# Hybrid decoder step on one core: a stacked fp32r product for the samples' new states in scan groups 2 to 4, weight halves made by ScalarE at a tile's begin, the gate's root at a tile's end

## What is computed

```
def ssd_scan(x, dt, A, B, C, h0):
    cum = jnp.cumsum(dt * A, axis=2)
    ...
    decay_to_end = jnp.exp(cum[:, :, -1:] - cum)
    chunk_states = jnp.einsum('bcjgn,bcjgr,bcjgrp->bcgrpn', B, decay_to_end * dt, x)
    chunk_decay = jnp.exp(cum[:, :, -1])
    def step(h, inp):
        d, s = inp
        return d[..., None, None] * h + s, h
```

```
    g = y.reshape(b, l, D_SSM) * jax.nn.silu(z.astype(jnp.float32))
    g = g.reshape(b, l, SSD_GROUPS, D_SSM // SSD_GROUPS)
    g = g * lax.rsqrt(jnp.mean(g * g, axis=-1, keepdims=True) + EPS)
```

## Time and profile before

| | us |
|---|---|
| median of 3 runs | 1800.54 (1800.42 to 1800.7) |
| profiled execution | 1800.39 |
| its span in the profile | 1798.8 |
| PE busy in the span | 1779.2 |
| DVE busy | 1088.6 |
| ACT busy | 770.2 |
| the 16 scan tiles, roughly | 546 to 755 of the span |

### The profile page before, as it was taken

The page is one execution under the profiler, slowest core; times in us unless marked ns, Lnnn a source line. Parts: engine busy times, 40 slices in busy tenths (PEclk is TensorE's granted clock), DMA queues, the critical chain, the costliest instruction groups (busy, mean ns, idle before and its releaser), DMA issues.

```text
span 1798.8 us, 34945 instructions
## 1 busy us (share of the span) xinstructions
PE 1779.2 (99%) x13213; PEld 1746.5 (97%) x13213; DVE 1088.6 (61%) x2004; ACT 770.2 (43%) x1139; POOL 453.2 (25%) x352
## 2 busy tenths in 40 slices
PE   8999999999999999999999999999999999999998
PEld 7999999999998898899899999999999999999998
DVE  5577887999788787865875333443434434344444
ACT  6443435555356565633443333333333333333442
POOL 1577776777651122222100000000000000000132
PEclk9999999999999999999999999999999999999999
DMA  8665554555545555564335444444444454444442
GB/s 252 176 189 153 145 157 139 149 152 153 153 144 165 161 177 163 163 215 152 117 123 166 156 140 140 157 156 155 140 140 153 156 158 140 140 151 158 154 143 87
DMA packets 287354, 278.42 MB, mean 155 GB/s; under 512 B 11639, under 2 KB 284767, under 8 KB 286385
## 3 DMA queue, kind: packets, MB, share of 16 engines
q1 hardware_dynamic: 249112, 247.87, 45.4%
q10 hardware_dynamic: 36496, 21.77, 4.1%
q0 software_dynamic: 1648, 7.43, 1.3%
HBM read 261.25 MB, written 17.22 MB: 155 GB/s over the span
## 4 chain that ended last, share of the span: by engine, by line
PE 94%; ACT 2%; DVE 2%; DMA 0%; issue 0%; ACTq 0%; SPq 0%; DVEq 0%
PE ps L1804 28%; PE ps L1806 28%; PE ps L1805 28%; PE ps L1863 1%; PE ps L2087 1%; PE ps L1865 1%; PE ps L1864 1%; PE ps L2060 1%; PE ps L2037 1%; PE ps L2131 1%; PE ps L2132 1%; PE ps L2133 1%; DMA xn<-in_x_prompt 0%; DVE mix L1671 0%; ACT wgt L988 0%
## 5 line engine op out<-in xcount | busy, mean ns | idle before, releaser
L1804 PE MATMUL ps<-ahi,whi 128*128 128x320 f32 x2304 | 717.8, 312 | 0.0
L1806 PE MATMUL ps<-ahi,wlo 128*128 128x320 f32 x2304 | 711.9, 309 | 0.0
L1805 PE MATMUL ps<-alo,whi 128*128 128x320 f32 x2304 | 711.8, 309 | 0.0
L677 ACT ACTIVATE whi<-raw 128x1024 fp32r<-128x1024 f32 (+1 forms) x467 | 479.5, 1048 | 448.6 <-PE ps L1806 382.9
L1205 DVE TENSOR_TENSOR wlo<-raw,whi 128x1024 fp32r<-128x1024 f32 x347 | 424.2, 1245 | 242.4 <-ACT whi L677 239.7
L1804 PEld LDWEIGHTS ps<-ahi,whi 128*128 128x128 f32 x2304 | 432.5, 188 | 1.7
L1805 PEld LDWEIGHTS ps<-alo,whi 128*128 128x128 f32 x2304 | 432.6, 188 | 0.5
L1806 PEld LDWEIGHTS ps<-ahi,wlo 128*128 128x128 f32 x2304 | 432.5, 188 | 0.0
L1804 PE MATMUL ps<-hhi,whi 128*128 128x320 f32 x1016 | 314.3, 309 | 0.0
L1806 PE MATMUL ps<-hhi,wlo 128*128 128x320 f32 x1016 | 313.9, 309 | 0.0
L1805 PE MATMUL ps<-hlo,whi 128*128 128x320 f32 x1016 | 313.9, 309 | 0.0
(11 more groups left out here) (316 smaller groups left out, 1626.3 us busy)
## 6 DMA issues: line engine op xcount, KB each, us to landing
raw<-in_w_in SPq DMA_DIRECT2D x144, 512.0 KB, 3.7
raw<-in_w_up SPq DMA_DIRECT2D x128, 512.0 KB, 4.5
raw<-in_w_down SPq DMA_DIRECT2D x128, 512.0 KB, 4.5
raw<-in_w_out SPq DMA_DIRECT2D x64, 512.0 KB, 3.8
h<-in_state_ssm ACTq DMA_DIRECT2D x16, 512.0 KB, 4.9
out<-hout ACTq DMA_DIRECT2D x16, 512.0 KB, 3.2
x_transposed<-xt ACTq DMA_DIRECT2D x1, 2560.0 KB, 10.1
xr<-x_transposed POOLq DMA_DIRECT2D x1, 2560.0 KB, 9.9
```

Of the source, the lines that this page charges most:

```text
L677: act.activation(whi[:, kq, :, 0:width], raw[:, kq, :, 0:width], ACT.Copy).then_inc(hi_done, 1)
L1804: pe.matmul(out, wh, hi[:, kk, :], start=(kk == 0), stop=False)
L1805: pe.matmul(out, wh, lo[:, kk, :], start=False, stop=False)
L1806: last = pe.matmul(out, wl, hi[:, kk, :], start=False, stop=(kk == NT - 1))
```

## The change

Four things change.

1. **The product.** For i ≥ 1 the samples' new states are formed by two fp32r matmuls with all 128 rows of contraction instead of two fp32 matmuls with 32 rows. The rows are stacked: `xq[h]` holds in rows 64 to 127 the high part of `xdd` (a rounded copy, ACT), in rows 32 to 63 the unrounded `xdd` of its half (ACT), in rows 0 to 31 the low part (a subtraction, DVE). `bq` holds, against these, the masked B, its low part and its high part. Each tile makes its `xq` (four ACT activations, two DVE subtractions); the `bq` of a group is made during the group before it, by ACT: `b_rows` at j = 1, `b_masked` (8 activations) at j = 2, `b_low` and `b_high` (8 and 2) at j = 3, with one subtraction by DVE at j = 2 and one more transpose on PE at j = 1. DVE's `bm` falls away for i ≥ 1.
2. **The weights.** From tile 1 on, ACT makes both high halves of a tile one behind the other at the tile's begin; before, the second came after the old states' copies. DVE's second low half stays where it was, and the two new subtractions stand behind it.
3. **The gate.** ACT copies the mean away (`gate_keep`) where it took the root, PE waits for that copy only, and `gate_root` moves behind the tile's second Exp. The early load of the root's table (`expect_root`) falls away here.
4. **The staging.** PE reads x and B from `xb` itself; `xst` and `bt` are gone.

```diff
@@ ACT @@
-            def stage_x(T):
...
-            def stage_b(i):
...
+            def b_rows(transposed):
+                act.activation(bts[64:P, :], transposed, ACT.Copy)
+                act.activation(bthi[64:P, :], transposed, ACT.Copy).then_inc(bts_ready, 1)
+
+            def b_masked(i):
+                act.wait_ge(bts_ready, i)
+                for b in range(NB):
+                    last = act.activation(bq[i % 2][64:P, b, :], bts[64:P, :], ACT.Copy, scale=blk[64:P, b:b + 1])
+                last.then_inc(bq_rows, 1)
+
+            def b_low(i):
+                act.wait_ge(btlo_done, i)
+                for b in range(NB):
+                    own = slice(64 + 32 * (b // 4), 96 + 32 * (b // 4))
+                    last = act.activation(bq[i % 2][32:64, b, :], btlo[own, :], ACT.Copy, scale=blk[own, b:b + 1])
+                last.then_inc(bq_ready, 1)
+
+            def b_high(i):
+                act.wait_ge(bq_rows, i)
+                for h in range(2):
+                    own = slice(64 + 32 * h, 96 + 32 * h)
+                    last = act.activation(bq[i % 2][0:32, 4 * h:4 * h + 4, :],
+                                          bq[i % 2][own, 4 * h:4 * h + 4, :].bitcast(F32), ACT.Copy)
+                last.then_inc(bq_ready, 1)
...
+            def gate_keep(g):
+                act.wait_ge(gn_mm, g + 1)
+                act.activation(gss[:, g, :], ps[:, 5, 0:TOK], ACT.Copy).then_inc(gn_kept, 1)
+
             def gate_root(g):
-                expect_root()
-                act.wait_ge(gn_mm, g + 1)
-                act.activation(gss[:, g, :], ps[:, 5, 0:TOK], ACT.Sqrt, bias=eps[:, 0:1], scale=float(GROUPS)
+                act.wait_ge(gn_kept, g + 1)
+                act.activation(gss[:, g, :], gss[:, g, :], ACT.Sqrt, bias=eps[:, 0:1], scale=float(GROUPS)
                                ).then_inc(rooted, 1)
...
                     ahead(Q_WC, i, 2 * j)
+                    if not first:
+                        ahead(Q_WC, i, 2 * j + 1)
...
+                    if i:
+                        act.wait_ge(xd_ready, T + 1)
+                        act.wait_ge(st_done, T)
+                        for h in range(2):
+                            act.activation(xq[h][64:P, :], xdd[64:P, 2, :], ACT.Copy).then_inc(xhi_done, 1)
+                        for h in range(2):
+                            last = act.activation(xq[h][32:64, :], xdd[64 + 32 * h:96 + 32 * h, 2, :], ACT.Copy)
+                        last.then_inc(xq_ready, 1)
...
                     if j == 1 and i >= 1:
-                        gate_root(i - 1)
-                    ahead(Q_WC, i, 2 * j + 1)
+                        gate_keep(i - 1)
...
                     decay(T, 1)
+                    if j == 1 and i < 3:
+                        act.wait_ge(bts_trans, i + 1)
+                        b_rows(ps[64:P, 3, TOK:448])
...
+                    if j == 1 and i >= 1:
+                        gate_root(i - 1)
+                    if j == 2 and i < 3:
+                        b_masked(i + 1)
+                    if j == 3 and i < 3:
+                        b_low(i + 1)
+                        b_high(i + 1)
                     store_h(T)
@@ DVE @@
+                    if j == 2 and i < 3:
+                        b_lowest(i + 1)
-                    if j == 0:
+                    if first:
                         dve.wait_ge(btok_ready, i + 1)
...
                     ahead(Q_WC, i, 0 if first else 2 * j + 1)
+                    if i:
+                        dve.wait_ge(xhi_done, 2 * T - 6)
+                        for h in range(2):
+                            own = slice(64 + 32 * h, 96 + 32 * h)
+                            last = dve.tensor_tensor(xq[h][0:32, :], xdd[own, 2, :], xq[h][own, :].bitcast(F32),
+                                                     ALU.subtract)
+                        last.then_inc(xq_ready, 1)
                     dve.wait_ge(exp_done, 2 * T + 2)
@@ PE @@
+                if j == 1 and i < 3:
+                    pe.wait_ge(exp_done, 2 * T + 1)
+                    pe.transpose(ps[:, 3, TOK:448], xb[:, NT + i + 1, TOK - P:TOK], ident[:]).then_inc(bts_trans, 1)
                 segment(T, 1, first)
...
                 if j == 1 and i:
-                    pe.wait_ge(rooted, 2 + i)
+                    pe.wait_ge(gn_kept, i)
...
+                else:
+                    pe.wait_ge(xq_ready, 2 * T - 6)
+                    pe.wait_ge(bq_ready, 2 * i)
+                    for h in range(2):
+                        pe.matmul(ps[:, 6 + h, :], xq[h][:], bq[i % 2][:, 4 * h:4 * h + 4, :], start=True, stop=True)
```

More of the change, by code:

```diff
@@ L152, in build @@
         sc = ar + 5120
-        bt = place("bt", [P, TOK], at=sc)
-        xst = place("xst", [P, TOK], at=sc + 320)
         btok = place("btok", [P, 3, P], at=sc + 640)
-        bm = place("bm", [P, NB, P], at=sc + 1024)
+        bts = place("bts", [P, P], at=sc)
+        bthi = place("bthi", [P, P], F32R, at=sc + 128)
+        btlo = place("btlo", [P, P], at=sc + 256)
+        xq = [place("xq0", [P, P], F32R, at=sc + 384), place("xq1", [P, P], F32R, at=sc + 512)]
+        bm = place("bm", [P, NB, P], at=ar + 12 * TOK)
+        bq = [place("bq0", [P, NB, P], F32R, at=ar + 12 * TOK), place("bq1", [P, NB, P], F32R, at=sc + 1024)]
         xd = place("xd", [P, 3, P], at=sc + 2048)
@@ L1055, in _ @@
             act.wait_ge(cn_done, 4)
-            stage_b(0)
-            stage_x(0)
             for i in range(3):
@@ L1066, in _ @@
                 ahead(Q_WS, 0, c)
+            gate_keep(3)
             gate_root(3)
@@ L1519, in gate_lo, with b_lowest @@
                                              ).then_inc(gact_ready, 1)
+            def b_lowest(i):
+                dve.wait_ge(bts_ready, i)
+                dve.tensor_tensor(btlo[64:P, :], bts[64:P, :], bthi[64:P, :].bitcast(F32), ALU.subtract
+                                  ).then_inc(btlo_done, 1)
             def wc(i):
@@ L1544, in wc @@
                     dve.tensor_tensor(wgt[:, 0, :], cb, wgt[:, 0, :], ALU.mult).then_inc(mixw_done, 1)
-                    if j == 0:
+                    if j == 2 and i < 3:
+                        b_lowest(i + 1)
+                    if first:
                         dve.wait_ge(btok_ready, i + 1)
-                        if not first:
-                            dve.wait_ge(st_done, 4 * i)
                         dve.tensor_tensor(bm[:], btok[:, 2, :].unsqueeze(1).to_broadcast([P, NB, P]),
@@ L2015, in scan_front @@
                     for c, off in enumerate((0, P, TOK - P)):
-                        last = pe.transpose(ps[:, 4, c * P:(c + 1) * P], bt[:, off:off + P], ident[:])
+                        last = pe.transpose(ps[:, 4, c * P:(c + 1) * P], xb[:, NT + i, off:off + P], ident[:])
                     last.then_inc(bt_trans, 1)
@@ L2020, in scan_front @@
                         hi = min((c + 1) * P, TOK)
-                        last = pe.matmul(ps[:, 2, c * P:hi], bt[:, off:off + P], xb[:, NT + GROUPS + i, c * P:hi],
+                        last = pe.matmul(ps[:, 2, c * P:hi], xb[:, NT + i, off:off + P], xb[:, NT + GROUPS + i, c * P:hi],
                                          start=True, stop=True)
@@ L2026, in scan_front @@
                     pe.wait_ge(pst_done, T)
-                pe.wait_ge(xst_ready, T + 1)
                 for c, off in enumerate((0, P, TOK - P)):
-                    last = pe.transpose(ps[:, 4, c * P:(c + 1) * P], xst[:, off:off + P], ident[:])
+                    last = pe.transpose(ps[:, 4, c * P:(c + 1) * P], xb[:, T, off:off + P], ident[:])
                 last.then_inc(xtile_trans, 1)
+                if j == 2 and i < 3:
+                    pe.wait_ge(bts_ready, i + 1)
                 segment(T, 0, first)
```

33 lines of the change are left out of this document (13 added, 20 removed).

## The result

| | changed kernel | before |
|---|---|---|
| median, us | 1809.87 (1807.26 to 1811.38, 6 runs) | 1800.6 (1800.42 to 1800.7, 6 runs) |
| ratio | 1.0051, 95% interval 1.0039 to 1.0063 | |
| profiled execution, its span | 1810.16, 1808.5 | 1800.39, 1798.8 |
| ACT busy in the span | 799.0 | 770.2 |

A forecast was written before the change was run, and what follows sets the result against it. PE bounds the kernel, with 94% of the chain that ended last. The terms -3.8 + 5.0 - 0.39 - 0.39 - 0.3 + 0.33 - 0.55 sum to -0.1, giving 1800.4 us; the range for 8 in 10 is 1797.2 to 1803.6.

The forecast's parts named there:

- PE waits 2.3 us: Tile 6 (j = 2): PE waits 2.3 us for `xq`, for a product that takes 0.45.
- Tile 4: -0.39: Tile 4 (j = 0): 0.39 us shorter.
- -0.15 each: Tiles 8 and 12 (j = 0): `ecb`, Exp and `wgt` 0.1 us earlier, saving 0.15 each, -0.3 together.
- until 655.53: End of j = 3 tiles: ACT finishes two halves at 655.53, then makes `btok`, which began at 655.52 before.
- rival B: ACT's queue becomes the bound, at `btok` and `ecb` in j = 0: +3.7 us, 1804.1; chance 0.07.
- +1.73, +1.73, +1.52: Tiles 6, 10, 14 (j = 2): longer by these us through the wait for `xq`, +5.0 together.
- -1.27 each: Tiles 5, 9, 13 (j = 1): `within` 1.27 us earlier without the table loads in front, -3.8 together.
- -0.39 each: Tiles 7, 11, 15 (j = 3): 0.39 us saved each, but 7 and 11 lose it waiting for `btok`.
- rival C: The stacked product is no faster, 1.06 us: 1804.8; chance 0.03.
- `within` at s + 2.76 at the earliest: Second `wgt` limits `within` in a tile: 0.39 us saved, not 0.61; the product could cost up to 0.67 unnoticed.
- A: Wait at j = 2 far smaller, 0.83 us, +0.2 instead of +1.7 a tile: 1796.0; chance 0.12.
- D: Each ACT table switch costs more than its load, 1.4 us more in tiles 6, 10, 14: 1804.6; chance 0.02.

The follow-up runs named there:

- e10: Changed kernel plus 26 bf16 matmuls with unread results directly ahead of the wait for `xq` in tiles 6, 10, 14: 1805.68 us, ratio 1.0028.
- e12: e8 with `b_high` moved from j = 3 to behind `b_masked` at j = 2: 1798.88 us, ratio 0.999.
- e9: Changed kernel with `xq` and `bq` made once, for tile 4, and used by all later tiles, leaving their new states uncomputed: 1794.47 us, ratio 0.9966.
- e8: Changed kernel with Exp's table loaded behind the root at j = 1 and the `xq` subtractions ahead of the second low half: 1800.34 us, ratio 0.9998.
- e4: Changed kernel without the stacked product: parts 2 to 4 with the earlier fp32 product and its `bm`: 1797.5 us, ratio 0.9983.
- e2: Changed kernel with a tiny Exp behind the root, loading Exp's table at the end of the j = 1 tile: 1805.1 us, ratio 1.0027.
- e1: Changed kernel plus 20 bf16 matmuls with unread results behind the wait for `hts` in tiles 6, 10, 14: 1806.93 us, ratio 1.0035.
- e6: Changed kernel with the gate's root and both table loads back at the front of the j = 1 tile: 1805.82 us, ratio 1.0029.
- e3: Changed kernel with DVE's two subtractions for `xq` ahead of the second low half: 1802.79 us, ratio 1.0012.

## Why the prediction was wrong, step by step

The prediction's terms against e10, which is the changed kernel with PE kept at full clock:

| tiles | predicted | e10 |
|---|---|---|
| j = 1: 5, 9, 13 (with two transposes) | -3.8 + 0.22 | -3.24 |
| j = 2: 6, 10, 14 | +5.0 | +6.23 |
| j = 0: 4, 8, 12 | -0.69 | +2.30 |
| j = 3: 7, 11, 15 | -0.39 | +0.06 |
| 0 to 3 (with a transpose) | -0.44 | -0.32 |
| sum | -0.1 | +5.0 |
| not in e10: nearly all the clock | none | +4.2 (after less e10) |

**The sum: TensorE at full clock throughout.** This is the largest failure, about 4 us. "PE waits 2.3 us" was added at its length, and what PE does behind such a wait was put at nothing, without a reason. The longest wait in the earlier trace rows is 0.9, so nothing in the rows could price one of 2.3; but then it was an operation that the trace of before doesn't show, and I gave it no bound. e10 shows the cost. Without this term the time would have been 1805.7, still above the range.

**j = 0, "Tile 4: -0.39", "-0.15 each", and `btok` "until 655.53".** Failed, 3.0 us, and it is rival B's place: in e10 PE waits 0.5 to 0.6 for `btok` in each of the three, and 0.6 for `hts` in tiles 8 and 12. Tile 4 was plainly miscounted: the ten activations stand in tile 3 too, since it has i < 3, so `btok` of tile 4 is as late as the others. The prices were low: `b_high` 0.64 for each in place of 0.52, `b_low` 2.57 for eight (652.98 to 655.55) in place of 2.4, and the four copies 1.18 (633.56 to 634.74 in tile 6) in place of 0.84, since the second kind don't overlap (0.31 from one to the next). In the changed kernel's profile the issue of a store took 1.48 besides. e12 shows that this place decides: `b_high` elsewhere gives back 1.46. I had B at 1804.1 with 0.07. My upper bound for it, +3.7, would have covered what came (its parts as written, 0.5 three times and 0.6 twice, with the gains of j = 0 given up, add to 3.4); the error was to take the low prices where I had counted no slack at all behind them.

**j = 2, "+1.73, +1.73, +1.52".** The mechanism is right, and its order is in the trace row by row; its size was 1.2 us short in all. In the changed kernel, against s, Exp came at -1.99 (I had -1.97) and DVE's `wgt` at -1.48 (-1.47). `btlo` follows it by 0.52 and not 0.41, the reciprocal follows `btlo` by 0.32 and not 0.21, the two subtractions take 0.57 and not 0.50, and the product begins 0.26 behind their end and not 0.06. In e10 that last step is 0.06; the product begins at s + 3.25, where I had 2.91, and `within` at s + 5.23, where I had 4.88.

**j = 1, "-1.27 each".** Right by e9 (-1.28, -1.27, -1.36). In the changed kernel 0.1 to 0.2 of it is lost: in tile 5 to a wait of 0.30 for `wgt`, as ACT's copies stand ahead of its Relu, in tiles 9 and 13 to waits of 0.29 and 0.39 for `xq`.

**j = 3, "-0.39 each".** I let `xq` be ready at s + 0.7; the product began at s + 1.20 (tile 7), and the gain was gone. With the subtractions first (e8) it is back in part, -0.25.

**The product itself, and rival C.** 0.61, not 0.45 (0.54 behind a wait), and harmless: under the 0.67 at which PE would notice. "`within` at s + 2.76 at the earliest" is exact.

**Which cases held.** A (a far smaller wait) didn't happen; D is refuted, and so is C. Of the 3.7 us of rival B 3.0 came, and in B's place, though its condition was only half met: the plain copies follow each other by 0.21 (64 rows) and 0.31 (32 rows), those with a scale by 0.29 and 0.32, not over 0.4. What no case had is the clock, so the range ended 3.7 us below the lowest run.

What stays open: why the issue of a store sometimes takes 1.5 to 2 us, and which of two equal waits the clock falls behind. The settled part is that the preparation of `xq` and `bq` is the whole loss (e9), and the clock about 4 us of it (e10).

## What to carry to other kernels

A faster instruction on the engine that bounds the kernel is worth what its slowest operand allows: lay out where each operand's last producer stands in its queue before pricing the instruction. Here 0.45 us saved on PE needed six more instructions on ACT and DVE in each tile and 21 for each group, and lost 15.4 us to them in all. Price a new standstill of TensorE above its length (here 1.4 us more for one of 2.8, where the clock fell), and try the parts of a change apart: three of the four here are worth 3.3 us together (e4).

## What was not expected of the hardware

- PE waiting 1.9 to 2.8 us for `xq` was followed by 3.4 or 6.8 us at a granted clock of 0.50 in some cases (tiles 6 and 14 of the changed kernel, tile 10 of e2, tile 7 of e1) and not in others (tile 10 of the changed kernel, 2.8; tile 6 of e2, 2.2; tile 11 of e1, 1.9). Nothing like it followed the waits of 1.6 in e6 and 1.7 in e3, in their profiles.
- The issue of one and the same store from ACT's queue takes mostly 0.42 to 0.46, and now and then 0.5 to 2.0; behind a long one ACT's next instruction waits. The kernel before has it too (1.62 once in its scan, 0.86 and 0.90 once each), and no wait of PE follows there. Its timeline of ACT:

```profile
718.58 1.62 ACTq L981 DMA_DIRECT2D out<-pst  x1
```

- ACT copies of 32 or 64 rows and 128 columns last 300 to 308 ns, and 383 to 386 with a scale from memory. The Trainium skill (ScalarE: Activation LUTs, What ACT_TABLE_LOAD costs) has 186 ns + 0.833 per column and about 93 more for an operand from memory, which is 293 and 386 for 128 columns and holds here for fewer rows too, within 5%. Of its overlap of about 93 ns between neighbours, the two copies of L1053 show 0.09 us (0.51 for two of 0.30), the two of L1055 none (0.62 for two of 0.31).
